# Next stage's first products placed among the last norm turns of three stage ends, with the first feed-forward weight sums

## What is computed

```python
for layer in range(2):                       # "even", then "odd"
    h = rms_norm(x, pre_norm[layer])
    m = even_mixer(h, ...) if layer == 0 else odd_mixer(h, ...)   # each ends in ... @ w_out
    x = x + rms_norm(m, post_norm[layer])
x = x + 0.5 * swiglu(rmsnorm(x, ffn1_norm), w_in, w_out)          # "ffn1"
x = x + hybrid_mixer(rmsnorm(x, mix_norm), ...)                   # "mix"
x = x + 0.5 * swiglu(rmsnorm(x, ffn2_norm), w_in, w_out)          # "ffn2"
return rmsnorm(x, final_norm)
# swiglu: a, b = split(x @ w_in);  (silu(a) * b) @ w_out
```

## Time and profile before

| | us |
|---|---|
| median of 3 runs (lowest to highest) | 2620.38 (2617.59 to 2620.84) |
| the profiled execution: its own time | 2620.42 |
| the profiled execution: span from first to last instruction | 2618.0 |
| PE busy | 2551.9 (97% of the span) |
| DVE busy | 1311.7 (50%) |
| ACT busy | 657.2 (25%) |
| chain that ended last: PE's share | 94% |
| mean granted PE clock | 0.991 |

### The profile page before, as it was taken

How to read it: one execution, slowest core, us unless ns; L and a number is a source line. 1 busy time by engine, 2 the same in 40 slices (tenths; PEclk the granted TensorE clock), 3 DMA queues, 4 the chain that set the end, 5 groups by cost and what they waited for, 6 DMA issues and landing times.

```text
span 2618.0 us, 31512 instructions
## 1 busy us (share of the span) xinstructions
PE 2551.9 (97%) x12699; PEld 1739.9 (66%) x12699; DVE 1311.7 (50%) x2535; ACT 657.2 (25%) x1485; POOL 60.3 (2%) x116
## 2 busy tenths in 40 slices
PE   8999999999999999999999999999999999999999
PEld 4487557566588888744545744555556775888886
DVE  6765342544444456425464446657473544444564
ACT  2123332264300000133344043525344002000001
POOL 0000000000000000000000010101020000000000
PEclk9999999999999999999999999999999999999999
DMA  4211222000222322221111221112112322223221
GB/s 158 66 63 65 91 73 85 33 33 33 65 66 96 97 82 80 80 78 52 65 66 67 66 95 65 57 57 81 65 48 96 122 97 65 97 65 97 97 74 71
DMA packets 121032, 196.86 MB, mean 75 GB/s; under 512 B 5212, under 2 KB 61336, under 8 KB 119992
## 3 DMA queue, kind: packets, MB, share of 16 engines
q1 hardware_dynamic: 118848, 180.52, 20.2%
q0 software_dynamic: 1344, 12.19, 1.2%
q10 hardware_dynamic: 696, 2.13, 0.2%
HBM read 187.49 MB, written 7.34 MB: 74 GB/s over the span
## 4 chain that ended last, share of the span: by engine, by line
PE 94%; DVE 2%; ACT 2%; issue 1%; DMA 0%; ACTq 0%; SPq 0%; DVEq 0%
PE psum L537 22%; PE psum L534 15%; PE psum L2426 10%; PE psum L2408 8%; PE psum L422 7%; PE psum L407 6%; PE psum L442 5%; PE psum L2460 3%; PE psum L459 2%; PE psum L1195 2%; PE psum L1175 1%; PE psum L466 1%; PE psum L395 1%; PE psum L1183 1%; PE psum L2352 1%
## 5 line engine op out<-in xcount | busy, mean ns | idle before, releaser
L590 DVE TENSOR_TENSOR arena<-arena,psum 128x512 f32<-128x512 f32 x197 | 135.3, 687 | 358.2 <-PE psum L537 304.7
L2426 PE MATMUL psum<-weight_ring,h_t 128*128 128x512 f32 x640 | 293.2, 601 | 1.9 <-ACT arena L2757 1.4
L537 PE MATMUL psum<-h_t,weight_ring 128*128 128x256 f32 x1120 | 254.0, 384 | 1.9 <-ACTq L2795 1.1
L537 PEld LDWEIGHTS psum<-h_t,weight_ring 128*128 128x128 f32 x1120 | 215.6, 193 | 32.8 <-ACTq L2795 1.3
L2408 PE MATMUL psum<-h_t,weight_ring 128*128 128x512 f32 x512 | 232.1, 595 | 0.3 <-issue 0.3
L534 PE MATMUL psum<-weight_ring,arena 128*128 128x256 f32 x992 | 220.5, 379 | 1.5 <-ACT arena L2885 1.5
L534 PEld LDWEIGHTS psum<-weight_ring,arena 128*128 128x128 f32 x992 | 188.3, 190 | 27.9 <-issue 2.4
L2426 PEld LDWEIGHTS psum<-weight_ring,h_t 128*128 128x128 f32 x640 | 116.8, 192 | 118.8 <-issue 116.1
L422 PE MATMUL psum<-h_t,weight_ring 128*128 128x512 f32 x416 | 180.1, 593 | 0.5 <-issue 0.5
L537 PE MATMUL psum<-arena 128*128 128x256 f32 x768 | 169.7, 379 | 0.0
L407 PE MATMUL psum<-weight_ring,h_t 128*128 128x512 f32 (+1 forms) x384 | 167.6, 594 | 0.8 <-DVEq L1733 0.8
(11 more groups left out here) (435 smaller groups left out, 3412.8 us busy)
## 6 DMA issues: line engine op xcount, KB each, us to landing
weight_ring<-in_ffn_w_in_dram SPq DMA_DIRECT2D x44, 1024.0 KB, 7.4
weight_ring<-in_w_in_dram SPq DMA_DIRECT2D x20, 2048.0 KB, 7.9
weight_ring<-in_ffn_w_out_dram SPq DMA_DIRECT2D x8, 2048.0 KB, 7.7
weight_ring<-in_w_in_even_dram SPq DMA_DIRECT2D x7, 2048.0 KB, 8.3
weight_ring<-in_w_in_odd_dram SPq DMA_DIRECT2D x5, 2048.0 KB, 7.8
weight_ring<-in_w_in_dram SPq DMA_DIRECT2D x8, 1024.0 KB, 7.2
weight_ring<-in_w_branch_gdn_dram SPq DMA_DIRECT2D x4, 2048.0 KB, 7.9
weight_ring<-in_ffn_w_out_dram SPq DMA_DIRECT2D x4, 1536.0 KB, 6.6
```

Source lines behind the costliest of these rows:

```text
L537: ins = pe.matmul(out, w, right[:, k, :], start=first, stop=last)
L590: ins = dve.tensor_tensor(out, other, bank, op)
L2426: last = pe.matmul(bank, act[:, k, t * P:(t + 1) * P], slot[:, k, :], start=(k == 0), stop=(k == KD - 1))
```

## The change

At the ends of the even, the odd and the hybrid stage ("mix") two pieces of the next stage's work are issued before the engines meet. The turn of tile 1 moves into the middle of tile 3's matmuls, at all four stage ends that have a following norm (the first feed-forward too). Tile 1's evictions move ahead of tile 3's chain in the programs of ACT and DVE. Behind the turn of tile 2 PE waits until tiles 0 and 1 are evicted, and then runs a first product: lat of tile 0 at the even end, p1 of the first feed-forward block at the other two. Behind the turn of tile 3 it runs a second, lat of tile 1 or p2, without waiting for the meeting. These two products take the banks that tile 1's turn used; lat of tiles 2 and 3, p3 and all later ones take theirs from the pool of all eight. The weight sums of the first feed-forward block are made on DVE at the stage end, two operations behind tile 1's scaled rows and two behind tile 2's; the feed-forward begins on DVE with the token sums.

```diff
-def pe_token_major(K, pe, key, act, n_cols, k0=0, nk=KD, col=0, blk=None, started=False, tiles=range(NT)):
+def pe_token_major(K, pe, key, act, n_cols, k0=0, nk=KD, col=0, blk=None, started=False, tiles=range(NT), among=None):
...
-        bank = K.next_bank((key, t))
+        bank = K.next_bank((key, t), among)
@@ pe_square_half
         for k in range(nk):
+            if half == t // 3 == 1 and k == nk // 2 and after:
+                after(t, True)
...
-SUMS_LATE = ("p1", "p2", "p3", "p5", "p6", "p7", "p4")
+SUMS_LATE = ("p3", "p5", "p6", "p7", "p4")
@@ pe_seven
-    K.weight_sums["pe"] += 1
-    for name in SUMS_LATE if late_sums else IN_TURN:
+    if not only or "p3" in only:
+        K.weight_sums["pe"] += 1
+    for name in only or IN_TURN:
         left, right = sides[name]
-        bank = pe_fresh(K, pe, (key, name))
+        bank = K.next_bank((key, name), among)
+        if K.turn((key, name)) > 1:
+            pe.wait_ge(K.free_of((key, name)), K.turn((key, name)) - 1)
@@ pe_next_norm
-    def after(t):
+    def after(t, middle=False):
         if t == 2:
             turn(0)
-        if t == 3:
-            for n in range(1, NT):
-                turn(n)
+        if t == 3 and middle:
+            turn(1)
+        if t == 3 and not middle:
+            turn(2)
+            if ahead:
+                for n in range(2):
+                    for half in range(2):
+                        pe.wait_ge(K.free_of((s, "next", n, half)), K.turn((s, "next", n, half)))
+                ahead[0]()
+            turn(3)
@@ dve_residual_tail (the like in dve_mix_out; without "between" in dve_half_tail; the evictions also in ACT's three)
+            if following and (half, t) == (1, 3):
+                dve_next_evict(K, dve, s, 1, norm_gain(K, following))
             dve.wait_ge(K.full_of(key), K.turn(key))
...
                 dve_next_tile(K, dve, s, t, following)
+                if t in (1, 2) and between:
+                    between(t)
                 if following and t == 2:
                     dve_next_evict(K, dve, s, 0, norm_gain(K, following))
     if following:
-        for t in range(1, NT):
+        for t in range(2, NT):
             dve_next_evict(K, dve, s, t, norm_gain(K, following))
...
+def pe_ffn_ahead(K, pe, s, before):
+    V = ffn_views(K)
+    blk = K.ffn_blocks[s]
+
+    def product(name, half):
+        among = (K.jobs[(before, "next", 1, half)][0],)
+        pe_seven(K, pe, (s, 0), blk, KD, K.h_t, V["weights0"], V["tokens"], False, 2, only=(name,), among=among)
+
+    def first():
+        assert K.next_block() == blk
+        pe.wait_ge(K.weight_landed[blk % SLOTS], K.landed_at[blk])
+        product("p1", 0)
+
+    return first, lambda: product("p2", 1)
...
+def dve_ffn_ahead(K, dve, s, t):
...
+    if t == 1:
+        dve.wait_ge(K.weight_landed[blk % SLOTS], K.landed_at[blk])
+        dve.tensor_tensor(s1, w21, w22, ALU.add).then_inc(K.one_more("dve"), 1)
+        dve.wait_ge(K.steps["dve"], K.step_n["dve"])
+        dve.tensor_tensor(w21, w11, w21, ALU.subtract).then_inc(K.one_more("dve"), 1)
+    else:
+        dve.tensor_tensor(s2, s1, w11, ALU.subtract).then_inc(K.one_more("dve"), 1)
+        dve.wait_ge(K.steps["dve"], K.step_n["dve"])
+        dve.tensor_tensor(s4, w12, s2, ALU.subtract).then_inc(K.weights_summed, 1)
@@ dve_ffn
-    dve_weight_sums(K, dve, first_blk, KD, V["weights0"], None, 2)
     dve_token_sums(K, dve, K.h_t, KD, V["tokens"])
@@ end of pe_even (pe_odd and pe_mix alike, with pe_ffn_ahead)
-    pe_square_early(K, pe, (s, "out"), K.h_t, 4, lambda: mixed(1), pe_next_norm(K, pe, s, True))
+    ahead = pe_odd_ahead(K, pe, "odd", s)
+    pe_square_early(K, pe, (s, "out"), K.h_t, 4, lambda: mixed(1), pe_next_norm(K, pe, s, True, ahead))
     pe.drain().then_inc(K.phase_met, 1)
+    ahead[1]()
     pe.wait_ge(K.phase_met, K.phase_end("pe"))
...
+def pe_odd_ahead(K, pe, s, before):
...
+        among = (K.jobs[(before, "next", 1, t)][0],)
+        pe_token_major(K, pe, (s, "lat"), K.h_t, M_QL + M_KL + M_R, blk=state["blk"], tiles=[t], among=among)
...
@@ pe_odd
-    pe_token_major(K, pe, (s, "lat"), K.h_t, M_QL + M_KL + M_R, blk=blk)
+    pe_token_major(K, pe, (s, "lat"), K.h_t, M_QL + M_KL + M_R, blk=K.block_n - 1, tiles=(2, 3))
```

More of the change, by code:

```diff
@@ L661, in scaled_rows, with pe_next_norm @@
     return K.carve(at, NT, D)[0]
-def pe_next_norm(K, pe, s, same_banks=False):
+def pe_next_norm(K, pe, s, same_banks=False, ahead=None):
     rows = scaled_rows(K, s)
@@ L769, in act_residual_tail @@
     for t in range(NT):
+        if following and t == 3:
+            act_next_evict(K, act, s, 1, norm_gain(K, following))
         act_next_square(K, act, s, 1, t, base + NT + t + 1, shifted + t + 1)
@@ L852, in pe_setup @@
     after = pe_next_norm(K, pe, "setup")
-    for t in range(2, NT):
-        after(t)
+    after(2)
+    after(3, True)
+    after(3)
     pe.drain().then_inc(K.phase_met, 1)
@@ L1284, in act_mix_out @@
             key = ((s, "out"), half, t)
+            if (half, t) == (1, 3):
+                act_next_evict(K, act, s, 1, gain)
             act.wait_ge(K.full_of(key), K.turn(key))
@@ L1295, in act_mix_out, with dve_mix_out @@
                     act_next_evict(K, act, s, 0, gain)
-    for t in range(1, NT):
+    for t in range(2, NT):
         act_next_evict(K, act, s, t, gain)
-def dve_mix_out(K, dve, s, proj):
+def dve_mix_out(K, dve, s, proj, between=None):
     gain = norm_gain(K, K.following[s])
@@ L1308, in dve_mix_out @@
     for t in range(NT):
+        if t == 3:
+            dve_next_evict(K, dve, s, 1, gain)
         rate = dve_rate(K, dve, 160, t)
@@ L1929, in pe_odd @@
         pe.wait_ge(K.free_of((s, "mixed", kt)), K.turn((s, "mixed", kt)))
-    pe_square_early(K, pe, (s, "out"), K.h_t, 6, mixed_rest, pe_next_norm(K, pe, s, True))
+    ahead = pe_ffn_ahead(K, pe, "ffn1", s)
+    pe_square_early(K, pe, (s, "out"), K.h_t, 6, mixed_rest, pe_next_norm(K, pe, s, True, ahead))
     pe.drain().then_inc(K.phase_met, 1)
+    ahead[1]()
     pe.wait_ge(K.phase_met, K.phase_end("pe"))
@@ L2141, in dve_odd @@
     dve_odd_gate(K, dve, s, V, 1)
-    dve_mix_out(K, dve, s, V["proj"])
+    dve_mix_out(K, dve, s, V["proj"], lambda t: dve_ffn_ahead(K, dve, "ffn1", t))
     dve.drain().then_inc(K.phase_met, 1)
@@ L2313, in pe_mix @@
     branches(0)
-    pe_square_early(K, pe, (s, "out"), K.h_t, 4, lambda: branches(1), pe_next_norm(K, pe, s, True))
+    ahead = pe_ffn_ahead(K, pe, "ffn2", s)
+    pe_square_early(K, pe, (s, "out"), K.h_t, 4, lambda: branches(1), pe_next_norm(K, pe, s, True, ahead))
     pe.drain().then_inc(K.phase_met, 1)
+    ahead[1]()
     pe.wait_ge(K.phase_met, K.phase_end("pe"))
```

22 lines of the change are left out of this document (15 added, 7 removed).

## The result

| | us |
|---|---|
| changed kernel, median of 4 runs (lowest to highest) | 2605.39 (2601.87 to 2606.79) |
| kernel before, beside it, median of 4 runs | 2619.76 (2617.59 to 2620.84) |
| ratio, with its 95% interval | 0.9944 (0.9932 to 0.9955) |
| profiled execution of the changed kernel: own time, span | 2601.87, 2599.6 |

The change is 14.4 us (0.55%) faster; 11.7 were forecast (from 2620.4 to 2608.7; the terms of the forecast add up to 11.8). The profiled execution is the fastest of the four. The page of the changed kernel, busy time of each engine in us, answers to the earlier trace rows: PE has 12 us less of busy time for the same number of instructions, so the same work ran less at half clock, and the span is 18.4 us shorter.

A forecast was written before the change was run, and what follows sets the result against it. PE, busy 2551.9 of 2618.0 us, bounds the kernel; its waits and half clock can be won. Terms 8.3 + 3.0 + 3.9 - 0.6 + 0.8 - 3.6 = 11.8 us give 2608.7 us, range 2603.5 to 2614.5.

The forecast's parts named there:

- Even end: Even stage end: lat of tile 0 fills the wait for tile 3's rows, lat of tile 2 waits 0.8 us; gain 8.3 us.
- Odd end: Odd stage end: tile 3's chain starts 1.9 us late on DVE, p3 waits 3.0 us for p2's bank; gain 3.0 us.
- Mix end: End of mix: p1 covers the wait for tile 3's rows and p3's bank is free; gain 3.9 us.
- End of ffn1: End of the first feed-forward: tile 3's chain starts 0.88 later with nothing placed into the wait; loss 0.6 us (0 to 0.9).
- Banks in mix: Inside mix: shifted bank order costs 0.6 us at the hf product, removes the gate's 1.38 us wait; net gain 0.8 us.
- Clock: New waits at p3 and ffn1's end: a fall to half clock at both, 1.8 us each, 3.6 lost (ends 0 and 8).
- No fall: Rival: the clock doesn't fall at either new wait, p3 or ffn1's end; 2605.1 us, chance 0.18.
- p3 without its bank wait: Rival, odd end: p3 doesn't wait for its bank, so 3.0 and its fall, 1.8, come back; 2603.9 us, chance 0.10.
- Half clock held long: Rival: half clock holds at both new waits as long as at the old even end, another 3 us each; 2614.7, chance 0.10.
- paced by DVE and ACT: Rival, three ends: token sums and evictions pace the next stage, half the gain (7.6) becomes waits elsewhere; 2616.3, chance 0.06.
- landing of the block: Rival: DVE's sums wait for the feed-forward block's landing, mix and odd ends each some 10 us later; 2628.7, chance 0.03.
- Transposes at half clock: Rival, four ends: the moved turn costs 1.97 us instead of 0.88, by the skill page's rule; 2613.1 us, chance 0.03.

The follow-up runs named there:

- other_bank: Changed kernel with the second product ahead (lat of tile 1, p2) taking the bank of tile 0's second half instead of tile 1's; 2599.14 us, ratio 0.9923.
- even_alone_back: Changed kernel with the two lat products put back behind the meeting at the even end alone, tile 1's turn staying moved; 2616.19 us, ratio 0.9982.
- turn_behind: Changed kernel with tile 1's turn back behind tile 3's matmuls at all four ends, products still ahead; 2608.35 us, ratio 0.9956.
- sums_later: Changed kernel with the second pair of ffn1's weight sums moved on DVE behind the last evictions of the odd end; 2607.38 us, ratio 0.9952.

## Why the prediction came out as it did

**Even end, forecast +8.3, measured +8.08.** Every step is in the rows: no wait for tile 3's rows, lat at full clock behind turn 2, lat of tile 2 waiting 0.69 us for ACT (0.8 forecast), no wait at cq. That this is a wait for the bank of lat of tile 1 is shown by other_bank, where it is gone. The experiment that puts this end back costs 9.28 us there, of which 1.20 is the moved turn's own price.

**Odd end, forecast +3.0, measured +3.64 without a fall and 1.97 to 2.21 with one.** The three waits came where the prediction put them, for the reasons that it gave, each a little shorter: 1.02 for 1.4, 0.92 for 1.55 and 2.62 for 3.0. The cause is one term, the delay of tile 3's chain on DVE. I had it start 1.9 us late. It starts 9.36 us behind tile 3's first matmul, where it was 8.12 (699.98 less 691.86, in the row of before below): 1.24 late, of which 0.88 is the turn. That the bank of p3 is the last limit is shown: with another bank p3 starts at once. Tile 3's matmuls at this end in the kernel before:

```profile
691.86 7.03 PE L442 MATMUL psum<-weight_ring,h_t 128*128 128x512 f32 x16
```

**Mix end, forecast +3.9, measured +3.93. End of ffn1, forecast -0.6, measured -0.65. Banks in mix, forecast +0.8, measured +0.86** (-0.68 and +1.54, from the rows at the two waits). These held to 0.1 us.

**Clock, forecast -3.6: the term that was too large.** The two new waits do draw the clock down, and a fall at p3 costs 1.4 to 1.7 us, near the 1.8 taken. But I took both as certain. p3's wait of 2.62 us had a fall in three of the five traces that have it (two of the changed kernel's three, even_alone_back; not turn_behind), the 1.98 us at ffn1's end in eight of ten. Also, before's profile carries falls that are no more certain than the new ones: the stretch to the odd end is 310.55 us there and 308.97 in the first trace of the changed kernel, with the same wait of 1.40 us in it. I left these constant. Without the clock the terms come to 8.08 + 3.64 + 3.93 - 0.65 + 0.86 = 15.9 us (15.4 forecast), or 2604.6 from 2620.42, where the forecast started, and 2603.9 from 2619.76, the median of the runs of before beside the changed kernel's. The profiled executions with both falls took 2607.21 and 2608.43, which is the forecast's case; the one with neither took 2601.87; the medians, 2605.4 and 2605.0, lie between. So the net of the clock in the median is some 0.4 to 1.5 us, depending on the start, not 3.6, and that is most of the 3.3 by which the forecast was high; the other terms, the odd end above all, make 0.5. The median lies in the range because the range reaches down past the rival without falls.

**The rivals.** "No fall", 2605.1, has the median's number, but not as a mechanism: the falls are there in two traces of three, and the execution without them, 2601.87, is 3.2 us faster still. Half clock that before's trace has elsewhere (near 590, 1190 and in part near 1575 us) is missing in it, and only a fall near 290 us is new. "p3 without its bank wait" was worth 3.0 and the fall; it measured 2.87 at the odd end, but the kernel as changed does have the wait. "Half clock held long" and "paced by DVE and ACT" show nowhere in the three traces. The sums were not held up by the landing of the block: on DVE, the first two at the mix end follow tile 1's rows at once (those rows start at 2176.38 and take 0.75 us, the first sum starts at 2177.04).

**Transposes at half clock.** The moved turns run in 1.04 us (0.87 from one start to the next instruction), and the stretches around the one at the even end, as above, have a granted clock of 1.00, which is 2.4 GHz:

```profile
344.00:346.00 2.00, 2.00 (x12) 1.00 0.00 0
...
348.00:350.00 2.00, 2.00 (x11) 1.00 0.00 0
```

The Trainium skill (TensorE: Matmul & The Clock Gate, Part 4) says that full clock doesn't engage for transposes; between matmuls these traces disagree, as they did before the change.

## What to carry to other kernels

When work is brought forward around a ring of buffers, replay the ring: the buffers that it is given, and the takes that it no longer makes, shift every later one. Here a collision with the buffer just given away cost 2.87 us and often a fall of the clock, and a bank whose reader is long done avoids both. A step moved ahead to make room for other work (turn 1) is worth its price only where there is such work; where there is none (the end of ffn1) leave it. Work of an engine belongs where that engine idles anyway, even if something queues behind it.

## What was not expected of the hardware

The same wait, in the same place of the same program, is followed by half clock in one execution and by full clock in the next (2.62 us at p3, 1.98 us at ffn1's end, 1.40 us inside the odd stage). Its length alone doesn't decide: in sums_later's trace a wait of 1.83 us was followed by half clock (p2 took 5.40 us), and the next one, of 3.33 us, was not (p3 took 3.69). Here are that trace's turn 3, p2 and p3, in order of time:

```profile
698.37 1.09 PE L683 MATMUL psum<-consts_sb,arena 128*128 128x128 f32 x8 [1.83 <-DVE arena L758]
...
699.57 5.40 PE L542 MATMUL psum<-h_t,weight_ring 128*128 128x256 f32 x16
708.30 3.69 PE L542 MATMUL psum<-h_t,arena 128*128 128x256 f32 x16 [3.33 <-issue]
```

The waits of 4.41 and of 5.14 to 5.63 us were followed by it in each of the four traces that have them, those of 1.11 at ffn1's end in neither of two. What decides in between stays open, and the changed kernel's executions reach from 2601.68 to 2608.43 us, a scatter larger than every term of the sum but one.
